# Tile 1's tokens and products behind two chunks of weights, the memory's loads on the weights' queue, products of ones between

## The chip, the cores and the metric

The kernel runs on one core of a Trainium2 chip. The metric is the device time of one execution in microseconds (us). The kernel before took a median of 922.51 us in three runs (921.90 to 922.72).

## The reference

The kernel computes two chained blocks of a transformer on 256 tokens of width 1024, in float32. The first block has two layers (a mixer of two kinds of attention, a SwiGLU with 2816 hidden columns, two layer norms in each). The second attends to its own tokens and to a memory of 256 rows. Only the first products and the memory's norm matter here:

```python
def _mixer_ab(h, w_in, q_norm, w_uq, kv_norm, w_ukv, sinks, w_out, cos, sin):
    B, S, _ = h.shape
    proj = jnp.einsum('bsd,df->bsf', h, w_in)
    c_q, c_kv, k_r, q_s, k_s, v_s = _split_cols(proj, AB_SPLITS)
    q = jnp.einsum('bsr,rf->bsf', _rms_norm(c_q, q_norm), w_uq).reshape(B, S, MLA_HEADS, MLA_NOPE + MLA_ROPE)
    ...

def first_block(x, ab_w_in, ...):
    for layer in range(DEPTH):
        ...
            mix = _mixer_ab(x, ab_w_in[i], ab_q_norm[i], ...)
        x = _layer_norm(DEEPNORM_ALPHA * x + mix, ln1_g[layer], ln1_b[layer])
        ffn = _swiglu(x, ffn_w_gate[layer], ffn_w_up[layer], ffn_w_down[layer])
        x = _layer_norm(DEEPNORM_ALPHA * x + ffn, ln2_g[layer], ln2_b[layer])
    return x

def second_block(x, mem, norm_g, mem_norm_g, ...):
        ...
        mem_n = rms_norm(mem, mem_norm_g[layer])
        out_c = memory_cross_attention(qc, mem_n, w_mem_kv[layer]) * jax.nn.silu(gc)
        ...
```

## The kernel before

SP's queue holds tile 0 of x, the identity, chunks 0 to 3, tile 1 of x (L515), then chunk 4 and the rest. GpSimd's queue holds what is needed later: behind chunk 3's high part the memory's gains (`mem_g`), the memory's rows (`mem`, 1024 KB), the low-rank gains (`gains`) and two head parameters; behind chunk 7's high part the table `swa` (1536 KB) and `rope`.

The memory's norm is made on ScalarE (L1403, L1404) and VectorE (L1845, L1846) while TensorE does the second step. On ScalarE it stands behind the high part of chunk 8. TensorE turns the normed memory's tile 0 behind chunk 7 and tile 1 behind chunk 8.

Of the kernel before, what the change touches and what calls it, by code (L numbers as in the profile page):

```python
# [28 lines left out]
P = 128  # L29
TT = 2  # L30
S = TT * P
D = 1024
# [232 lines left out]
def build_program(nc, d, out):  # L265
    with ExitStack() as ctx:
# [236 lines left out]
        def read(name, steps):  # L503

            u = PRODUCTS[name].u0 + steps - 1
            return acc_free[u % 2], TT * (u // 2 + 1)

        block = ctx.enter_context(nc.Block())

        @block.sync
        def _(sp):

            def load_x(t):
                sp.dma_start(x[:, t, :], d["x"][t * P:(t + 1) * P, :]).then_inc(loaded[f"x{t}"], 16)  # L515

            load_x(0)
# [19 lines left out]
            for g in PRODUCTS.values():  # L537
                if g.name[:2] == "up":
                    users = PRODUCTS["ukv" if g.name == "up0" else "down0"]
                    sp.wait_ge(chunk_used, users.c0 + users.steps * users.kc // users.kp)  # L540
                for n in range(g.steps * g.kc // g.kp):
                    if g.c0 + n:
                        load_chunk(g, n)
                    else:
                        for m, landed in enumerate((first_staged, staged[STAGE[0]])):
                            cut = slice(m * FIRST, (m + 1) * FIRST)
                            sp.dma_start(stage_of(0, WIDTH[0])[:, cut], d["w_ab_in"][0][:, cut]).then_inc(landed, 16)
                    if g.c0 + n == NS - 1:
                        load_x(1)
            for t in range(TT):  # L550
                for j in range(2):
# [9 lines left out]
        def _(pool):  # L561
            def load(name, dst, src):
                pool.dma_start(dst, src).then_inc(loaded[name], 16)

            def row(src, n):
                return bass.AP(tensor=src.tensor, offset=src.offset, ap=[[0, P], [1, n]])

            pool.memset(no_mask[:, :], 0.0).then_inc(constants_set, 1)
            pool.wait_ge(hi_done, NS)
            load("mem_g", row_g[:, :], row(d["mem_norm_g"], D))  # L570
            load("mem", mem_x, d["mem"].rearrange("(t p) n -> p t n", t=TT))
            load("gains", gains, row(d["gains"], Q_RANK + KV_RANK))
            load("heads", head_par[:, :, :].rearrange("p a h -> p (a h)"), row(d["head_par"], 16))
# [73 lines left out]
        def _(pe):  # L647
# [5 lines left out]
            def turn_part(part, name, src, ready):  # L653
# [7 lines left out]
                last.then_inc(turned, 1)  # L661

            def step(g, j, hi, lo, k0=0, turned_by=None, between=None, second=None):

                u, cps = g.u0 + j, g.kc // g.kp
                pair = u % 2
                passes = [(t,) for t in range(TT)] if second else [tuple(range(TT))]
                for tiles in passes:
                    if second:  # L670
                        second(tiles[0])
                    if u >= 2:

                        pe.wait_ge(acc_free[pair], 2 * (u // 2) - (tiles == (0,)))
                    for m in range(cps):
                        n = j * cps + m
# [554 lines left out]
        def _(act):  # L1231
# [224 lines left out]
            act.copy(w_hi(0, 0, FIRST), stage_of(0, FIRST)).then_inc(first_hi, 1)  # L1456
            turn_part(last, "x0")
            act.wait_ge(staged[STAGE[0]], 16)
            act.copy(w_hi(0, FIRST, FIRST), stage_of(0, WIDTH[0])[:, FIRST:]).then_inc(hi_done, 1)  # L1459
            done["chunks"] = 1  # L1460
            split_to(NS)
            turn("x0", xt_hi, 0, [1])

# [160 lines left out]
        def _(dve):  # L1624
# [348 lines left out]
            done["chunks"] = 1  # L1973
            turn_part(last, xt_hi, xt_lo, 0, "x0")
            split_to(NS)
            turn("x0", xt_hi, xt_lo, 0, [1])

# [340 lines left out]
```

## Time and profile before

| | |
|---|---|
| Median of 3 runs | 922.51 us (921.90 to 922.72) |
| The profiled execution | 924.75 us |
| Its span | 922.6 us |
| TensorE busy | 911.3 us, 99% of the span |
| VectorE busy | 608.7 us, 66% |
| ScalarE busy | 508.4 us, 55% |
| DMA, mean | 184 GB/s |

The rows of the trace are given in the section below. PE is TensorE, PEld its loading of stationary operands, DVE is VectorE, ACT ScalarE, POOL GpSimd and SP the engine that issues most transfers. A row of a timeline has the start and the duration in us, and a group "x8" covers eight records. For a product the duration runs to the modelled end of its pipeline, so in a dense stretch the distance from start to start is the one that counts. What stands in brackets is the idle time before it and what ended it. In a row of transfers the last number is the time from issue to landing in us.

### The profile page before, as it was taken

The numbers are of one execution on the slowest core, as the hardware profiler recorded it, in microseconds if no ns is written. First come the engines' busy times: TensorE is split into PE (matmuls) and PEld (weight loads), VectorE is DVE, ScalarE is ACT, GpSimd is POOL, SyncE is SP. The second block draws the span as 40 slices with busy tenths as digits, with TensorE's granted clock in tenths as the row PEclk, the third lists the DMA queues.
The fourth block names the chain that finished last, engine by engine and source line by source line (L and its number), as shares of the span: only waits on it lengthen the run. The fifth ranks groups of instructions, "written<-read, shape, count | busy, mean of one in ns | idle before, by whom it ended". The sixth has DMA issues, their size and how long they took to land.

```text
span 922.6 us, 12818 instructions
## 1 busy us (share of the span) xinstructions
PE 911.3 (99%) x4766; PEld 765.2 (83%) x4766; DVE 608.7 (66%) x1003; ACT 508.4 (55%) x819; POOL 36.4 (4%) x53
## 2 busy tenths in 40 slices
PE   8999999999999999999999999999999999999997
PEld 6888878888888898877888888887888888888876
DVE  3788687666662766778766666376656577574665
ACT  4876664555552456666455555355457574655444
POOL 1100024100000001000000000001000000000000
PEclk9999999999999999999999999999999999999999
DMA  8664466755574668444755557454564565545651
GB/s 293 238 220 121 122 226 194 262 183 185 192 246 131 146 172 256 137 155 166 256 176 187 195 189 245 125 198 142 185 204 137 160 195 167 163 152 189 197 174 64
DMA packets 72556, 169.39 MB, mean 184 GB/s; under 512 B 11304, under 2 KB 33216, under 8 KB 71856
## 3 DMA queue, kind: packets, MB, share of 16 engines
q1 hardware_dynamic: 69536, 155.83, 52.2%
q0 software_dynamic: 2816, 12.48, 4.1%
q8 instruction: 39, 0.64, 0.3%
q10 hardware_dynamic: 144, 0.26, 0.1%
q14 instruction: 21, 0.17, 0.1%
HBM read 167.49 MB, written 1.06 MB: 183 GB/s over the span
## 4 chain that ended last, share of the span: by engine, by line
PE 95%; DVE 2%; ACT 1%; DMA 1%; issue 0%; SPq 0%; ACTq 0%; DVEq 0%
PE psum L740 21%; PE psum L927 14%; PE psum L693 8%; PE psum L688 8%; PE psum L690 8%; PE psum L931 7%; PE psum L960 7%; PE psum L965 3%; PE psum L851 3%; PE psum L861 3%; PE psum L855 3%; PE psum L1062 2%; PE psum L1093 1%; PE psum L660 1%; PE psum L1076 1%; PE psum L1018 1%
## 5 line engine op out<-in xcount | busy, mean ns | idle before, releaser
L1636 DVE TENSOR_TENSOR base_lo<-stage,base_hi 128x1024 fp32r<-128x1024 f32 (+3 forms) x222 | 262.1, 1204 | 95.1 <-ACT base_hi L1245 94.2
L1245 ACT CAST base_hi<-stage 128x1024 fp32r<-128x1024 f32 (+3 forms) x222 | 223.8, 1035 | 52.4 <-PE psum L693 25.3
L1636 DVE TENSOR_TENSOR extra_lo<-stage,extra_hi 128x1024 fp32r<-128x1024 f32 (+1 forms) x68 | 80.0, 1202 | 47.5 <-ACT extra_hi L1245 47.4
L688 PE MATMUL psum<-base_hi,xt 128*128 128x512 f32 (+2 forms) x272 | 107.8, 396 | 1.6 <-ACT base_hi L1459 0.7
L690 PE MATMUL psum<-base_lo,xt 128*128 128x512 f32 (+2 forms) x272 | 105.2, 387 | 1.2 <-DVE base_lo L1636 0.7
L693 PE MATMUL psum<-base_hi,xt 128*128 128x512 f32 (+2 forms) x272 | 105.3, 387 | 0.0
L1245 ACT CAST extra_hi<-stage 128x1024 fp32r<-128x1024 f32 (+1 forms) x68 | 68.1, 1030 | 49.3 <-PE psum L740 33.5
L740 PE MATMUL psum<-base_hi,ht 128*128 128x512 f32 x288 | 87.3, 393 | 0.0
L927 PE MATMUL psum<-xt,extra_hi 128*128 128x512 f32 x320 | 87.3, 394 | 0.0
L960 PE MATMUL psum<-xt,base_hi 128*128 128x512 f32 x240 | 76.5, 403 | 0.0
L927 PE MATMUL psum<-xt,base_hi 128*128 128x512 f32 x256 | 69.7, 394 | 0.0
L740 PEld LDWEIGHTS psum<-base_hi,ht 128*128 128x128 f32 x288 | 53.7, 188 | 11.8 <-issue 0.5
L927 PEld LDWEIGHTS psum<-xt,extra_hi 128*128 128x128 f32 x320 | 55.4, 189 | 8.0
L688 PEld LDWEIGHTS psum<-base_hi,xt 128*128 128x128 f32 x272 | 51.5, 189 | 12.3 <-ACT base_hi L1459 1.1
L690 PEld LDWEIGHTS psum<-base_lo,xt 128*128 128x128 f32 x272 | 51.6, 190 | 11.7 <-DVE base_lo L1636 1.2
L693 PEld LDWEIGHTS psum<-base_hi,xt 128*128 128x128 f32 x272 | 51.4, 189 | 10.0 <-DVE xt L1677 0.4
L1436 ACT COPY qk_t<-psum 128x512 f32<-128x512 f32 x18 | 10.6, 587 | 84.4 <-PE psum L927 84.4
L1926 DVE TENSOR_TENSOR qk_t<-qk_t,psum 128x512 f32<-128x512 f32 x18 | 12.4, 687 | 62.9 <-ACT qk_t L1436 62.9
L931 PEld LDWEIGHTS psum<-xt,extra_lo 128*128 128x128 f32 x320 | 47.7, 189 | 5.9
L740 PE MATMUL psum<-base_lo,ht 128*128 128x512 f32 x144 | 50.8, 391 | 0.2 <-DVE base_lo L1636 0.2
L965 PEld LDWEIGHTS psum<-xt,base_lo 128*128 128x128 f32 x240 | 42.9, 188 | 9.2
L927 PEld LDWEIGHTS psum<-xt,base_hi 128*128 128x128 f32 x256 | 44.3, 189 | 6.5
(243 smaller groups left out, 1548.2 us busy)
## 6 DMA issues: line engine op xcount, KB each, us to landing
stage<-in_w_up SPq DMA_DIRECT2D x80, 512.0 KB, 4.5
stage<-in_w_down SPq DMA_DIRECT2D x44, 512.0 KB, 4.5
stage<-in_w_in_a SPq DMA_DIRECT2D x22, 512.0 KB, 4.9
stage<-in_w_cd_in SPq DMA_DIRECT2D x16, 512.0 KB, 4.7
stage<-in_w_in_b SPq DMA_DIRECT2D x12, 512.0 KB, 3.6
stage<-in_w_ab_in SPq DMA_DIRECT2D x11, 480.0 KB, 6.8
ln_par<-in_ln POOLq DMA_DIRECT2D x4, 1024.0 KB, 6.6
stage<-in_w_ab_out SPq DMA_DIRECT2D x8, 512.0 KB, 3.7
```

The lines of the kernel that those rows point to most:

```text
L688: pe.matmul(acc, ah, wh, start=(k == 0), stop=False)
L690: pe.matmul(acc, ah, wl, start=False, stop=False)
L693: last = pe.matmul(acc, al, wh, start=False, stop=(k == g.kc - 1))
L740: last = pe.matmul(psum[:, 2 * ((g.u0 + half) % 2) + t, :], a, w(c, half * 512, 512), start=(k == 0 and w is w_hi and a is ah), stop=summed)
L851: pe.matmul(acc, ah, w_hi(c, at, g.n), start=(k == 0), stop=False)
L855: pe.matmul(acc, al, w_hi(c, at, g.n), start=False, stop=False)
L927: last = pe.matmul(acc, w_hi(c, at, P), xt[:, k, :, :].rearrange("p a n -> p (a n)"), start=(k == 0), stop=(k == g.kc - 1))
L931: last = pe.matmul(acc[:, 0:S], w_lo(c, at, P), xt_hi[:, k, :], start=False, stop=False)
L960: last = pe.matmul(acc, w_hi(c, at, P), joint[:, k, :, :].rearrange("p a n -> p (a n)"), start=(k == 0), stop=(k == g.kc - 1))
L965: last = pe.matmul(acc[:, 0:S], w_lo(c, at, P), joint[:, k, 0, :], start=False, stop=False)
L1245: act.copy(w_hi(c, 0, w), stage_of(c, w)).then_inc(hi_done, 1)
L1636: dve.tensor_tensor(w_lo(c, 0, w), stage_of(c, w), w_hi(c, 0, w).bitcast(F32), ALU.subtract).then_inc(lo_done, 1)
```

## The change

Three parts, all within the first 30 us.

1. On SP's queue the load of tile 1 moves from behind chunk 3 to behind chunk 1. The three loads `mem_g`, `mem` and `gains` leave GpSimd's queue and stand on SP's behind chunk 7.
2. TensorE does chunks 0 and 1 for tile 0, turns tile 1, does chunks 0 and 1 for tile 1 (`early`), and then chunks 2 and 3 for both tiles together. Within `early` the products of the high weights (high and low tokens) stand ahead of those of the low weights, for each half of chunk 0 and for the whole of chunk 1. For tile 0 seven products of ones stand between: 0, 1 and 1 ahead of the low products of the three groups, 3, 2 and 0 behind them.
3. On ScalarE and VectorE the turn of tile 0's second half moves behind chunk 0 on ScalarE, and the two halves of tile 1's turn stand ahead of chunks 2 and 3 instead of behind chunk 3.

The whole diff:

```diff
--- before.py
+++ after.py
@@ -505,6 +505,9 @@
             u = PRODUCTS[name].u0 + steps - 1
             return acc_free[u % 2], TT * (u // 2 + 1)
 
+        def row(src, n):
+            return bass.AP(tensor=src.tensor, offset=src.offset, ap=[[0, P], [1, n]])
+
         block = ctx.enter_context(nc.Block())
 
 
@@ -513,6 +516,13 @@
 
             def load_x(t):
                 sp.dma_start(x[:, t, :], d["x"][t * P:(t + 1) * P, :]).then_inc(loaded[f"x{t}"], 16)
+
+            def load_memory():
+                for name, dst, src in (
+                        ("mem_g", row_g[:, :], row(d["mem_norm_g"], D)),
+                        ("mem", mem_x, d["mem"].rearrange("(t p) n -> p t n", t=TT)),
+                        ("gains", gains, row(d["gains"], Q_RANK + KV_RANK))):
+                    sp.dma_start(dst, src).then_inc(loaded[name], 16)
 
             load_x(0)
             sp.dma_start(ident[:, :], d["ident"]).then_inc(loaded["ident"], 16)
@@ -545,8 +555,10 @@
                         for m, landed in enumerate((first_staged, staged[STAGE[0]])):
                             cut = slice(m * FIRST, (m + 1) * FIRST)
                             sp.dma_start(stage_of(0, WIDTH[0])[:, cut], d["w_ab_in"][0][:, cut]).then_inc(landed, 16)
-                    if g.c0 + n == NS - 1:
+                    if g.c0 + n == 1:
                         load_x(1)
+                    if g.c0 + n == 2 * NS - 1:
+                        load_memory()
             for t in range(TT):
                 for j in range(2):
                     cut = slice(j * 512, (j + 1) * 512)
@@ -562,14 +574,8 @@
             def load(name, dst, src):
                 pool.dma_start(dst, src).then_inc(loaded[name], 16)
 
-            def row(src, n):
-                return bass.AP(tensor=src.tensor, offset=src.offset, ap=[[0, P], [1, n]])
-
             pool.memset(no_mask[:, :], 0.0).then_inc(constants_set, 1)
             pool.wait_ge(hi_done, NS)
-            load("mem_g", row_g[:, :], row(d["mem_norm_g"], D))
-            load("mem", mem_x, d["mem"].rearrange("(t p) n -> p t n", t=TT))
-            load("gains", gains, row(d["gains"], Q_RANK + KV_RANK))
             load("heads", head_par[:, :, :].rearrange("p a h -> p (a h)"), row(d["head_par"], 16))
             pool.wait_ge(hi_done, 2 * NS)
             load("swa", table, d["swa"])
@@ -660,19 +666,44 @@
                     last = pe.transpose(turn_bank(name, g)[:, k * P:(k + 1) * P], src(k0 + k, t), ident[:, :])
                 last.then_inc(turned, 1)
 
+            def early(g, pair, t, turned_by):
+
+                acc = psum[:, 2 * pair + t, 0:g.n]
+                for c, group, before_lows, behind in ((0, (0,), 0, 3), (0, (1,), 1, 2), (1, (0, 1), 1, 0)):
+                    ks = [(kk, c * g.kp + kk) for kk in group]
+                    at = lambda k: (slice(None), k, slice(t * P, (t + 1) * P))
+                    for kk, k in ks:
+                        pe.wait_ge(*((hi_done, c + 1) if k else (first_hi, 1)))
+                        pe.wait_ge(turn_hi, turned_at(turned_by, t, k))
+                        pe.matmul(acc, xt_hi[at(k)], w_hi(c, kk * g.n, g.n), start=(k == 0), stop=False)
+                    for kk, k in ks:
+                        pe.wait_ge(turn_lo, turned_at(turned_by, t, k))
+                        pe.matmul(acc, xt_lo[at(k)], w_hi(c, kk * g.n, g.n), start=False, stop=False)
+                    if t == 0:
+                        ones_by_ones(before_lows)
+                    for kk, k in ks:
+                        pe.wait_ge(*((lo_done, c + 1) if k else (first_lo, 1)))
+                        last = pe.matmul(acc, xt_hi[at(k)], w_lo(c, kk * g.n, g.n), start=False, stop=False)
+                    if t == 0:
+                        ones_by_ones(behind)
+                    elif ks[-1][0] == g.kp - 1:
+                        last.then_inc(chunk_used, 1)
+
             def step(g, j, hi, lo, k0=0, turned_by=None, between=None, second=None):
 
 
                 u, cps = g.u0 + j, g.kc // g.kp
                 pair = u % 2
-                passes = [(t,) for t in range(TT)] if second else [tuple(range(TT))]
-                for tiles in passes:
-                    if second:
-                        second(tiles[0])
+                passes = [(tuple(range(TT)), range(cps))]
+                if second:
+                    passes = [(tuple(range(TT)), range(2, cps))]
+                    for t in range(TT):
+                        second(t)
+                        early(g, pair, t, turned_by)
+                for tiles, chunks in passes:
                     if u >= 2:
-
-                        pe.wait_ge(acc_free[pair], 2 * (u // 2) - (tiles == (0,)))
-                    for m in range(cps):
+                        pe.wait_ge(acc_free[pair], 2 * (u // 2))
+                    for m in chunks:
                         n = j * cps + m
                         c = g.c0 + n
                         for kk in range(g.kp):
@@ -1454,12 +1485,16 @@
             turn_part(first, "x0")
             act.wait_ge(first_staged, 16)
             act.copy(w_hi(0, 0, FIRST), stage_of(0, FIRST)).then_inc(first_hi, 1)
-            turn_part(last, "x0")
             act.wait_ge(staged[STAGE[0]], 16)
             act.copy(w_hi(0, FIRST, FIRST), stage_of(0, WIDTH[0])[:, FIRST:]).then_inc(hi_done, 1)
             done["chunks"] = 1
+            turn_part(last, "x0")
+            split_to(2)
+            first, last = turn_parts("x0", [1])
+            turn_part(first, "x0")
+            split_to(3)
+            turn_part(last, "x0")
             split_to(NS)
-            turn("x0", xt_hi, 0, [1])
 
             def memory_norm():
                 act.wait_ge(constants_set, 3)
@@ -1972,8 +2007,12 @@
             split_first(1).then_inc(lo_done, 1)
             done["chunks"] = 1
             turn_part(last, xt_hi, xt_lo, 0, "x0")
+            split_to(2)
+            first, last = turn_parts("x0", [1])
+            turn_part(first, xt_hi, xt_lo, 0, "x0")
+            split_to(3)
+            turn_part(last, xt_hi, xt_lo, 0, "x0")
             split_to(NS)
-            turn("x0", xt_hi, xt_lo, 0, [1])
 
             def memory_norm():
                 dve.wait_ge(loaded["mem_g"], 16)
```

On TensorE before, the first step from its first product on; `base_hi` and `base_lo` are the weights' parts, `xt` the tokens, and the third row of each three takes the tokens' low part:

```order
L688 MATMUL psum<-base_hi,xt 128x480 [waits turn_hi,first_hi]
L690 MATMUL psum<-base_lo,xt 128x480 [waits first_lo]
L693 MATMUL psum<-base_hi,xt 128x480 [waits turn_lo]
L688 MATMUL psum<-base_hi,xt 128x480 [waits turn_hi,hi_done]
L690 MATMUL psum<-base_lo,xt 128x480 [waits lo_done]
L693 MATMUL psum<-base_hi,xt 128x480 [waits turn_lo]
...
L660 MATMUL psum<-ident,x 128x128 [waits turn_lo,loaded_x1]
L660 MATMUL psum<-ident,x 128x128 x3
```

On TensorE now, the same place; `qk_t` holds the ones:

```order
L678 MATMUL psum<-base_hi,xt 128x480 [waits turn_hi,first_hi]
L681 MATMUL psum<-base_hi,xt 128x480 [waits turn_lo]
L686 MATMUL psum<-base_lo,xt 128x480 [waits first_lo]
L1153 MATMUL psum<-qk_t 128x128 x3
...
L678 MATMUL psum<-base_hi,xt 128x480 [waits turn_hi,hi_done] x2
L681 MATMUL psum<-base_hi,xt 128x480 [waits turn_lo] x2
L1153 MATMUL psum<-qk_t 128x128
L686 MATMUL psum<-base_lo,xt 128x480 [waits lo_done] x2
L666 MATMUL psum<-ident,x 128x128 [waits turn_lo,loaded_x1]
L666 MATMUL psum<-ident,x 128x128 x3
```

The transposes of tile 1 stand behind 12 products instead of 24, and four products that need no low part of chunk 1 stand ahead of the wait for it.

On ScalarE before, from tile 0's first turn to the splitting of chunk 3:

```order
L1280 CAST xt<-psum 128x4x128 [waits turned]
L1456 CAST base_hi<-stage 128x480 [waits first_staged]
L1280 CAST xt<-psum 128x4x128 [waits turned]
L1459 CAST base_hi<-stage 128x480 [waits staged0]
L1245 CAST base_hi<-stage 128x960 [waits staged1]
L1245 CAST base_hi<-stage 128x960 [waits staged2]
L1245 CAST base_hi<-stage 128x960 [waits staged3]
L1280 CAST xt<-psum 128x4x128 [waits turned] x2
```

On ScalarE now:

```order
L1311 CAST xt<-psum 128x4x128 [waits turned]
L1487 CAST base_hi<-stage 128x480 [waits first_staged]
L1489 CAST base_hi<-stage 128x480 [waits staged0]
L1311 CAST xt<-psum 128x4x128 [waits turned]
L1276 CAST base_hi<-stage 128x960 [waits staged1]
L1311 CAST xt<-psum 128x4x128 [waits turned]
L1276 CAST base_hi<-stage 128x960 [waits staged2]
L1311 CAST xt<-psum 128x4x128 [waits turned]
L1276 CAST base_hi<-stage 128x960 [waits staged3]
```

Chunk 2 now stands behind the turn of tile 1's first half, and chunk 3 behind that of its second.

On SP now, the head of the queue (before, tile 1 stood behind the three chunks after chunk 0, and no row of the memory's was there):

```order
L557 DMA stage<-in_w_ab_in 128x480 x2
L545 DMA stage<-in_w_ab_in 128x960
L518 DMA x<-in_x 128x1024
L545 DMA stage<-in_w_ab_in 128x960 x2
L545 DMA stage<-in_w_ab_in 128x960 [waits lo_done] x4
L525 DMA row_g<-in_mem_norm_g 128x1024
L525 DMA arena<-in_mem 128x2x1024
L525 DMA arena<-in_gains 128x640
L545 DMA stage<-in_w_ab_in 128x960 [waits lo_done] x4
```

Chunk 8, the first of the last row, stands behind the memory's three loads.

## Rows read from the trace of the kernel before

**Rows 1.** The page, part 1 and the first line of part 4.

```profile
PE 911.3 (99%) x4766; PEld 765.2 (83%) x4766; DVE 608.7 (66%) x1003; ACT 508.4 (55%) x819; POOL 36.4 (4%) x53
...
PE 95%; DVE 2%; ACT 1%; DMA 1%; issue 0%; SPq 0%; ACTq 0%; DVEq 0%
```

**Rows 2.** TensorE's waits from 30 us on: total, times, longest, in us.

```profile
PE psum L1002 <- DVE pair_probs L1751: 0.6, 1, 0.6
PE psum L1043 <- DVE row_g L1986: 0.6, 1, 0.6
```

**Rows 3.** Windows: length, busy time of each engine, then PEclk, DMA share, GB/s.

```profile
4.70:7.00 2.30, 2.02 (x14) 1.68 (x13) 0.80 (x2) 1.42 (x3) 0.00 (x0) 1.00 0.98 310
7.00:12.00 5.00, 2.83 (x8) 1.22 (x8) 3.15 (x5) 2.85 (x5) 0.00 (x0) 0.99 0.99 365
12.00:15.40 3.40, 3.40 (x10) 2.83 (x10) 2.04 (x2) 0.86 (x1) 2.23 (x4) 0.51 0.79 261
...
12.00:18.00 6.00, 6.00 (x25) 5.04 (x24) 2.04 (x2) 1.13 (x2) 2.48 (x4) 0.72 0.73 254
```

**Rows 4.** Timeline of TensorE: start and duration in us, then idle before.

```profile
5.82 0.61 PE L1122 MATMUL psum<-qk_t 128*128 128x128 f32 x4
...
8.91 0.48 PE L688 MATMUL psum<-base_hi,xt 128*128 128x480 f32 x1 [0.69 <-ACT base_hi L1459]
9.60 0.48 PE L690 MATMUL psum<-base_lo,xt 128*128 128x480 f32 x1 [0.21 <-DVE base_lo L1965]
...
11.75 0.64 PE L690 MATMUL psum<-base_lo,xt 128*128 128x480 f32 x1 [0.71 <-DVE base_lo L1636]
...
17.10 1.04 PE L660 MATMUL psum<-ident,x 128*128 128x128 f32 x8
18.47 0.46 PE L688 MATMUL psum<-base_hi,xt 128*128 128x480 f32 x1 [0.33 <-ACT xt L1280]
...
19.10 0.49 PE L693 MATMUL psum<-base_hi,xt 128*128 128x480 f32 x1
19.43 0.38 PE L688 MATMUL psum<-base_hi,xt 128*128 128x480 f32 x1
...
24.01 0.37 PE L688 MATMUL psum<-base_hi,xt 128*128 128x480 f32 x1
...
34.39 1.04 PE L660 MATMUL psum<-ident,arena 128*128 128x128 f32 x8
```

**Rows 5.** Timeline of ScalarE: chunk 1, tile 1's turn, chunk 8.

```profile
9.51 0.99 ACT L1245 CAST base_hi<-stage 128x960 fp32r<-128x960 f32 x1 [0.65 <-DMA stage<-in_w_ab_in]
...
17.74 1.07 ACT L1280 CAST xt<-psum 128x512 fp32r<-128x512 f32 x2 [4.87 <-PE psum L660]
...
27.41 1.00 ACT L1245 CAST base_hi<-stage 128x960 fp32r<-128x960 f32 x1 [0.40 <-DMA stage<-in_w_ab_in]
```

**Rows 6.** Timeline of VectorE: chunks 1 to 3, tile 1's turn, the memory's first norm.

```profile
10.53 3.52 DVE L1636 TENSOR_TENSOR base_lo<-stage,base_hi 128x960 fp32r<-128x960 f32 x3 [0.39 <-ACT base_hi L1245]
18.35 1.29 DVE L1677 TENSOR_TENSOR xt<-psum,xt 128x512 fp32r<-128x512 f32 x2 [4.30 <-ACT xt L1280]
...
30.09 1.28 DVE L1846 SCALAR_TENSOR_TENSOR arena<-arena,rms_st,row_g 128x1024 f32<-128x1024 f32 x1
```

**Rows 7.** Issues on SP at 2.66, 4.08, 12.91, 27.34: KB, us to landing.

```profile
stage<-in_w_ab_in SPq DMA_DIRECT2D x1, 480.0 KB, 6.8
...
x<-in_x SPq DMA_DIRECT2D x1, 512.0 KB, 9.0
...
stage<-in_w_ab_in SPq DMA_DIRECT2D x1, 480.0 KB, 7.8
...
stage<-in_w_ab_in SPq DMA_DIRECT2D x1, 480.0 KB, 3.7
```

**Rows 8.** Timeline of GpSimd: issues of mem_norm_g and swa.

```profile
13.17 0.67 POOL L563 DMA_DIRECT2D row_g<-in_mem_norm_g  x1 [12.06 <-ACT base_hi L1245]
...
27.31 0.53 POOL L563 DMA_DIRECT2D arena<-in_swa  x1 [11.65 <-ACT base_hi L1245]
```

## Prediction

> **What bounds the kernel now.** I read part 1 of the page, then the chain that ended last, then the windows and timelines of the first 60 us, where every edit lies. TensorE is busy for 911.3 of 922.6 us and makes up 95% of the chain [rows 1]: a microsecond of its work brought forward shortens the run, if nothing behind it waits for something else. After 30 us its waits are 1.8 us in all, the longest 0.6 us each [rows 2] (three groups of 0.2 us each are not shown). So there is nothing to win there, and little that would swallow a gain. The first 24 us are different. TensorE records 2.83 busy us of 5.00 between 7 and 12 us. Then, from 12.0 to 15.4 us, it is busy throughout at a granted clock of 0.51, half speed, that is 1.2 instead of 2.4 GHz. Before 7 us it was busy 2.02 of 2.30 us at 1.00 [rows 3]. Up to 11.75 us the products wait for weights: 0.69, 0.21 and 0.71 us at 8.91, 9.60 and 11.75 us [rows 4]. The waits end when ScalarE has rounded a landed chunk and VectorE has made its rest.
>
> The measure is the start of the second step of ab_in, 24.01 us [rows 4]. A product at full speed takes (34.39 - 24.01)/48 = 0.216 us start to start [rows 4].
>
> **The first step in the old order.** At 11.75 us, when the low part of chunk 1 is there, 7 of the step's 48 products are done and 41 are left. The 17 of tile 0 take 17.10 - 11.75 = 5.35 us [rows 4]; at full speed they would take 17 x 0.216 = 3.68 us, and 0.11 us more since the first after a wait is followed at 0.33 and not 0.22 us (19.10 to 19.43) [rows 4]. So the half clock costs 5.35 - 3.79 = 1.56 us. Then eight transposes until tile 1's first product: 18.47 - 17.10 = 1.37 us. Its 24 products take 24.01 - 18.47 = 5.54 us, 0.35 us over 24 x 0.216 [rows 4].
>
> **The same step in the new order, part by part.**
> - High parts ahead of low, tile 0. In chunk 1 the two high products and the two of the tokens' rest need no low weights, so four and not one stand before the wait of 11.75 us. Nothing on VectorE moves ahead of that low part: it starts chunk 1 at 10.53 us as now [rows 6]. Ten products are done, 38 are left: 3 x 0.216 = 0.65 us saved.
> - Products of ones: seven, between the products, behind waits of tile 0. Two of them now are 4 records in 0.61 us [rows 4], so 0.3 us each at most. Three stand before 8.91, one before 9.60, two and one around chunk 1. The four early products of chunk 1 start from 10.55 to 11.2 us; the product of ones behind them is over by 11.75 us. I cost them at nothing; were each late by as much as its wait doesn't cover, the last alone would count, since each stage restarts from a weight: 0 to 0.3 us. What they may give is the clock. Busy time before the fall was 57% (2.83 of 5.00). With three more products and up to 7 x 0.3 = 2.1 us of ones it would be nearer the 88% of 4.7 to 7 us, which was followed by no fall [rows 3]. Bounds: 0 if the clock falls all the same, 1.56 if it does not fall. I take 1.56.
> - Tile 1's tokens behind chunk 1. The issue at 4.08 us landed 9.0 us later, at 13.1 us. Chunk 1 (2.66 + 6.8) landed at 9.46 us, so chunks 2, 3 and this tile came in 3.64 us, 1472 KB at 414 GB/s [rows 7]. Moved ahead of two of them the tile is there at about 10.8 us. Chunks 2 and 3 are 1.3 us later, 12.0 and 13.1. The transposes can start once the two low products of chunk 1 are out: 11.75 + 0.33 + 0.22 = 12.30 us; they don't wait for the load.
> - Tile 1's turn. By the distances of now (17.74, 18.47 and 19.10 against 17.10) [rows 4, 5] ScalarE copies the first half at 12.94, the first product starts at 13.67 and the one with the rest of the tokens at 14.30 us. Today a product with the low weights stands between these two; now the rest is needed second. It costs 14.30 - 13.67 - 0.216 = 0.41 and 0.11 behind it, 0.53 (unrounded) in place of 0.35: 0.18 us lost.
> - ScalarE and VectorE queues. ScalarE: tile 0's second half moves behind chunk 0 (a gap before the row of 9.51 us takes it [rows 5]), and chunk 2 stands behind the first turn: 13.5 to 14.4, turn to 14.9, chunk 3 to 15.9 us, against 12.86 us now. VectorE follows with 1.16 us a chunk (3.52 for three) and 0.65 a turn [rows 6]: chunk 2's rest at 15.65, turn 16.25, chunk 3's 17.35 us. TensorE reaches chunk 2 at 14.63 + 10 x 0.216 = 16.8 and chunk 3 at 19.4 us; both are covered, by 1.1 us or more.
>
> Sum: 11.75 + 38 x 0.216 + 0.11 + 1.37 + 0.53 = 21.98 us for the start of the second step; 24.01 - 21.98 = 2.03 = 0.65 + 1.56 - 0.18. The profiled execution took 924.75 us with a span of 922.6; the sum gives 920.6 for the span and 922.7 for that execution. It stood 2.2 us over the median of 922.51, and I take the difference off the median: **920.5 us**.
>
> On the clock there is a rule that speaks against carrying the 1.56 over. The Trainium skill, "TensorE: Matmul & The Clock Gate", Part 1, says that the gate runs free and isn't started by the kernel, so that the number of slow products differs from run to run. One trace can't show that; three times within 0.8 us don't contradict it. By the rule half of the fall, an estimate, might be what the median holds, and the sum would be 921.3.
>
> **The memory's three loads.** They leave GpSimd's queue (issued at 13.2 to 14.5 us) for the weights' queue, behind chunk 7 and ahead of chunk 8. Chunk 7's issue waits for VectorE's chunk 3, so 17.4 us, and its landing is 3.7 us later by the row of an issue into an idle queue [rows 7], 21.1 us. SP then issues mem_norm_g, mem, gains and chunk 8 without a wait that counts. Queued behind them are chunk 8 (480 KB) and all later weights. ScalarE must split chunk 8 before it squares mem: now chunk 8 lands at 27.41 and the first tile of mem is normed at 30.09 + 1.28 = 31.37 us, 3.96 us later [rows 5, 6]. TensorE takes it at 34.39 now [rows 4], 32.36 then. So chunk 8 may land as late as 28.4 us. What stands before its landing is 512 + 1024 + 320 + 480 = 2336 KB, 2.39 MB. At 414 GB/s it lands at 26.9 us; at 254 GB/s, the mean of 12 to 18 us [rows 3], at 30.5. How fast a row spread over 128 partitions goes on this queue no row shows. With the 1504 KB of mem and chunk 8 at 414 and the 832 KB of the two spread rows at 254 it is 28.2 us. I take 27.5, between the nearer two, as the weights' queue ran at 414 with several transfers waiting: in time by 0.9 us, cost 0. Bounds: 0 and 2.1 us.
>
> The Trainium skill, "DMA: Bandwidth & Descriptors", Specifications, puts a core's share of HBM at about 358 GB/s; the 414 GB/s above lies over it, and the measurement decides. By the page's figure chunk 8 would land at 27.8 us, an estimate, still in time.
>
> **The rivals.**
> - The clock falls all the same. For it: transposes and two waits at 12.3 to 14.3 us leave holes. Against: much more work before. Two low products, the transposes, and about five products would run at half speed, but the 0.6 us wait for the turn hides some: 0.3 us on the transposes and 0.4 to 0.7 on products. Less saved, 0.7 to 1.0: 921.2 to 921.5.
> - Chunk 8 is late. For it: one load issued at 12.91 us beside GpSimd's took 7.8 us [rows 7], and spread rows are untried here. It costs what it lands behind 28.4 us, and the transposes of mem after chunk 7 wait: with 28.7 to 30.5 us, 0.3 to 2.1 us, so 920.8 to 922.6.
> - Slower than before. The same place, with swa on top: chunk 7's split at 24.9 us (now 2.4 us later) lets GpSimd issue 1536 KB [rows 8], which then shares with chunk 8. At 254 GB/s the three loads end at 28.6 us and chunk 8 at half that rate 3.9 us later, 32.5: 4.1 us of stall, 924.6 us. It decides from a landing at 30.4 us on. Against it: 414 GB/s with a full queue.
> - The edit gives more: if the two waits around the turn shorten, or the fall costs more in other runs, 919.8.
>
> **How the numbers follow.** No change means within 0.2%, 1.85 us, so 920.66 to 924.36; it is about what a measurement here can tell. The forecast is near that edge.
> - Forecast, 920.5, own range 920.0 to 921.0: 0.48, of which 0.34 below the edge and 0.14 within.
> - Clock falls: 0.14, all within.
> - Chunk 8 late: 0.22, 0.02 below and 0.20 within.
> - Slower: 0.05. More gain: 0.07, below. The remaining 0.04, within: the gain is swallowed by later waits, up to the 1.8 us of [rows 2].
>
> Faster 0.43, same 0.52, slower 0.05. The range, 919.7 to 922.4, leaves out the slower rival and the ends of the others.
>
> **What would show it.** In the new profile: tile 1's eight transposes start near 12.3 us instead of 17.10; the granted clock stays 1.00 from 12 to 15.4 us and products follow at 0.22 us; tile 1's second product starts 0.6 us behind its first; the second step starts near 22.0 us. ScalarE's ninth chunk starts before 28.4 us, and the first transposes of mem stand right behind chunk 7's last product, near 32.4 us. A clock of 0.5 anywhere before 20 us speaks for the first rival; a gap before the transposes of mem for the second or third. The forecast is wrong if the second step starts later than 22.6 us, or if it starts near 22.0 and the span isn't shorter by about as much.

## The result, and the profile after

The changed kernel takes 925.24 us (median of 8 runs, 923.95 to 926.75) against 922.34 for the kernel before (8 runs, 921.73 to 922.98). The ratio is 1.0028, with a 95% interval of 1.0017 to 1.0038: slower, and outside the range of the prediction. The profiled execution took 924.95 us with a span of 923.0. One later execution of the kernel before took 1292 us at a granted clock of 0.655; no number below contains it.

The windows of the changed kernel: length, busy time of each engine, granted clock, DMA share, GB/s.

```profile
7.00:12.00 5.00, 5.00 (x33) 4.29 (x32) 2.74 (x4) 1.87 (x4) 0.00 (x0) 1.00 1.03 409
12.00:15.40 3.40, 2.89 (x14) 2.12 (x13) 2.68 (x4) 3.40 (x5) 0.34 (x1) 1.00 0.45 171
17.00:19.00 2.00, 2.00 (x10) 1.71 (x10) 1.37 (x2) 0.00 (x1) 0.00 (x0) 1.00 0.67 117
24.00:34.40 10.40, 8.90 (x45) 7.50 (x44) 5.29 (x7) 4.40 (x8) 1.07 (x2) 1.00 1.02 415
34.40:60.00 25.60, 23.95 (x155) 20.13 (x154) 22.01 (x60) 20.78 (x56) 3.51 (x6) 1.00 0.63 222
```

What TensorE does in the first 24 us is what was forecast. From 7 to 12 us it is busy for 5.00 of 5.00 us where it was busy for 2.83, and from 12 to 15.4 us the clock stays at 1.00 where it was at 0.51 [rows 3]. TensorE's timeline of the same trace (start, duration, form, idle before) stands against [rows 4]:

```profile
11.26 1.04 PE L666 MATMUL psum<-ident,x 128*128 128x128 f32 x8
12.63 0.46 PE L678 MATMUL psum<-base_hi,xt 128*128 128x480 f32 x1 [0.33 <-ACT xt L1311]
13.26 0.49 PE L681 MATMUL psum<-base_hi,xt 128*128 128x480 f32 x1 [0.18 <-DVE xt L1712]
...
20.96 0.38 PE L719 MATMUL psum<-base_hi,xt 128*128 128x480 f32 x1
...
33.04 1.09 PE L666 MATMUL psum<-ident,arena 128*128 128x128 f32 x8 [1.50 <-DVE arena L1881]
36.94 1.22 PE L666 MATMUL psum<-ident,arena 128*128 128x128 f32 x8 [0.19 <-DVE ht L1712]
40.63 0.82 PE L666 MATMUL psum<-ident,arena 128*128 128x128 f32 x6
41.82 0.49 PE L721 MATMUL psum<-base_lo,xt 128*128 128x480 f32 x1 [0.16 <-DVE base_lo L1671]
45.31 0.41 PE L1074 MATMUL psum<-ident,arena 128*128 128x128 f32 x2 [0.82 <-DVE row_g L2025]
```

The second step starts at 20.96 us, 3.05 us earlier than before. Of these, 1.03 us are no gain: chunk 1 happened to be rounded at 8.48 us in this execution, at 9.51 in the old one. Counted from there it is 12.48 us, by the forecast 21.98 - 9.51 = 12.47. But from 24 us on TensorE is busy for 1.5 us less of 10.4, and the memory's transposes, which had no wait, wait for 1.50 us. What holds them stands on ScalarE. Its timeline, start and duration:

```profile
21.16 1.02 ACT L1453 COPY arena<-psum 128x480 f32<-128x480 f32 x2 [4.15 <-PE psum L724]
22.06 1.90 ACT L1276 CAST base_hi<-stage 128x960 fp32r<-128x960 f32 x2
29.02 1.00 ACT L1276 CAST base_hi<-stage 128x960 fp32r<-128x960 f32 x1 [5.06 <-DMA stage<-in_w_ab_in]
29.92 1.06 ACT L1434 ACTIVATE arena<-arena 128x1024 f32<-128x1024 f32 x1
...
33.67 1.00 ACT L1276 CAST base_hi<-stage 128x960 fp32r<-128x960 f32 x1 [0.91 <-DMA stage<-in_w_ab_in]
34.57 1.01 ACT L1453 COPY arena<-psum 128x480 f32<-128x480 f32 x2
```

ScalarE sits idle for 5.06 us until chunk 8 lands at 29.0 us, where the squares of mem are queued behind it. Then it waits again, 0.91 us for chunk 9, with the copy of the second step's result and the turn of mem queued behind that. In the chain that ended last DMA's share rose from 1 to 4% [rows 1]:

```profile
PE 90%; DMA 4%; DVE 3%; ACT 2%; issue 1%; SPq 0%; ACTq 0%; DVEq 0%
```

The issues on SP, with KB and us to landing, are chunk 6 (14.59 us), chunk 7 (16.26), mem_norm_g, mem, gains and chunk 8 (18.2):

```profile
stage<-in_w_ab_in SPq DMA_DIRECT2D x1, 480.0 KB, 3.4
...
stage<-in_w_ab_in SPq DMA_DIRECT2D x1, 480.0 KB, 5.7
...
row_g<-in_mem_norm_g SPq DMA_DIRECT2D x1, 512.0 KB, 7.3
...
arena<-in_mem SPq DMA_DIRECT2D x1, 1024.0 KB, 9.4
...
arena<-in_gains SPq DMA_DIRECT2D x1, 320.0 KB, 9.8
...
stage<-in_w_ab_in SPq DMA_DIRECT2D x1, 480.0 KB, 10.8
```

Chunk 7 needs 5.7 us where 3.7 was assumed [rows 7]: it is down at 22.0 us and not at 20.0. In two microseconds of this time the transfers ran at 117 GB/s (window 17 to 19). The four behind it need 7.0 us for 2.39 MB, 340 GB/s.

### The profile page after: what moved, and what is told of

Its sections match the earlier page's. It is cut to its first block, busy times and chain, and to the rows that moved or that the text cites. A ratio compares the mean times of both kernels' runs of the same rounds, so it can differ in the third digit from the quotient of the medians.

```text
span 923.0 us, 12846 instructions
## 1 busy us (share of the span) xinstructions
PE 911.1 (99%) x4780; PEld 765.5 (83%) x4780; DVE 608.8 (66%) x1003; ACT 508.1 (55%) x819; POOL 34.1 (4%) x50
## 4 chain that ended last, share of the span: by engine, by line
PE 90%; DMA 4%; DVE 3%; ACT 2%; issue 1%; SPq 0%; ACTq 0%; DVEq 0%
PE psum L771 21%; PE psum L958 14%; PE psum L962 7%; PE psum L719 7%; PE psum L724 7%; PE psum L721 7%; PE psum L991 6%; PE psum L996 3%; PE psum L882 3%; PE psum L886 3%; PE psum L892 3%; DMA stage<-in_w_cd_in 2%; DVE base_lo L1671 2%; PE psum L1093 2%; DMA stage<-in_w_ab_in 2%; PE psum L1124 1%
## 5 line engine op out<-in xcount | busy, mean ns | idle before, releaser
L719 PE MATMUL psum<-base_hi,xt 128*128 128x512 f32 (+2 forms) x264 | 103.8, 393 | 0.0
L721 PE MATMUL psum<-base_lo,xt 128*128 128x512 f32 (+2 forms) x264 | 101.4, 384 | 0.2 <-DVE base_lo L1671 0.2
L724 PE MATMUL psum<-base_hi,xt 128*128 128x512 f32 (+2 forms) x264 | 101.5, 384 | 0.0
L721 PEld LDWEIGHTS psum<-base_lo,xt 128*128 128x128 f32 x264 | 49.6, 188 | 9.7 <-DVE base_lo L1671 0.6
L719 PEld LDWEIGHTS psum<-base_hi,xt 128*128 128x128 f32 x264 | 49.6, 188 | 9.4 <-issue 0.4
L724 PEld LDWEIGHTS psum<-base_hi,xt 128*128 128x128 f32 x264 | 49.6, 188 | 9.4
```

Source lines behind the costliest of these rows:

```text
L719: pe.matmul(acc, ah, wh, start=(k == 0), stop=False)
L721: pe.matmul(acc, ah, wl, start=False, stop=False)
L724: last = pe.matmul(acc, al, wh, start=False, stop=(k == g.kc - 1))
```

## The experiments

To compare executions I count from the start of chunk 1's rounding on ScalarE. In the profiles it lies between 7.97 and 9.51 us, and in the two of the unchanged kernel at 9.51 and 8.56, so most of this comes from nothing in the code. **D1** runs to the copy of the first step's result (ScalarE), **D2** to the memory's first transposes, **D3** to the transposes at L1074 of the changed kernel (45.31 us above). "Wait" is TensorE's before D2. The last column is the median less that of the kernel before in the same batch. `head_par` is the 8 KB load of the head parameters on GpSimd's queue, issued behind chunk 3's high part.

| kernel | D1 | D2 | wait | D3 | median | difference |
|---|---|---|---|---|---|---|
| before, again | 14.71 | 24.89 | 0 | 35.82 | 922.48 | -0.20 |
| e2 old order, memory behind chunk 7 | 13.16 | 23.33 | 0 | 34.28 | 922.76 | +0.08 |
| e8 old order, memory behind chunk 3 | 14.70 | 24.88 | 0 | 35.83 | 922.85 | +0.28 |
| the change | 12.68 | 24.56 | 1.50 | 36.83 | 925.24 | +2.90 |
| e3 no ones | 12.64 | 24.64 | 1.66 | 36.94 | 925.25 | +2.57 |
| e5 swa later | 13.07 | 24.45 | 0.99 | 35.69 | 924.00 | +1.42 |
| e11 head_par later | 13.14 | 23.90 | 0.41 | 35.14 | 924.06 | +1.73 |
| e1 memory on GpSimd | 12.98 | 23.20 | 0 | 34.14 | 923.02 | +0.34 |
| e7 memory behind chunk 8 | 13.01 | 23.24 | 0 | 35.17 | 922.66 | +0.08 |
| e4 memory behind chunk 3 | 12.72 | 22.90 | 0 | 33.85 | 922.54 | -0.04 |
| e6 the same, no ones | 12.67 | 22.90 | 0 | 33.85 | 922.11 | -0.47 |
| e10 e6 once more | 12.68 | 22.90 | 0 | 33.85 | 922.20 | -0.37 |
| e9 e6, swa later | 12.66 | 22.84 | 0 | 33.78 | 922.21 | -0.36 |
| e12 e9, head_par later | 12.68 | 22.85 | 0 | 33.80 | 921.72 | -0.61 |

**The kernel before, unchanged.** 

> The kernel before, unchanged, to see its spans and clocks over several executions. Theory A (the profiled execution of before was a slow one: its span of 922.6 us holds a clock fall of 1.56 us that most executions have less of): most spans are 920 to 921 us and the granted clock of several is above 0.997. Theory B (all executions have the fall): the clocks are alike at 0.997 and the spans 920 us differ from 922.6 for another reason. Both expect a ratio of 1.000.

Measured 922.48 us (ratio 0.9996, 0.9987 to 1.0005). Theory A holds: ten of the twelve spans are 920.0 to 920.7 us, with mean clocks of 0.998 to 1.000; the other two are 922.0 and 923.0 us, with 0.997. The profiled execution is one of these two and had the fall, the stretch at about half clock, again:

```profile
12.00:15.40 3.40, 3.40 (x11) 2.86 (x10) 1.14 (x1) 0.00 (x0) 2.49 (x4) 0.58 0.83 280
```

**The three loads back on GpSimd.** `load_memory()` leaves SP; the three `load(...)` lines return ahead of `load("heads", ...)`.

> The changed kernel with the memory's three loads back on GpSimd's queue behind chunk 3's high part. Late-memory theory (chunk 8 landed at 29.0 us behind the three loads, the memory's norm came 1.5 us late for TensorE and all of the first step's 3 us were gone by 34 us): chunk 8 lands before 25 us, no wait before the transposes of the memory, and the time is 920 to 922.5 us. Rival (what is lost lies after 34 us, in the chains of the first heads, or in how the products are ordered): within 0.5 us of the changed kernel, 925 us.

Measured 923.02 us (1.0003, 0.9994 to 1.0011). The wait of 1.50 us is gone, and with it 2.6 of the 2.9 us of difference: the place of the loads made most of the loss. It isn't faster than before, though.

**Only the three loads moved, old order.**

```diff
 (kernel before)
+                    if g.c0 + n == 2 * NS - 1:
+                        load_memory()
```

> The kernel before with only the three loads moved to the weights' queue behind chunk 7, whose issue is at 14.1 us there. Late-memory theory in its narrow form (the loads hurt because chunk 7's issue is late and the first step ends early): no harm here, 922.3 us within 0.7, since chunk 8 is issued at 22.6 us anyway. Rival (the spread rows are slow on this queue and hold the weights up): chunk 8 lands at 28 us or later and the time is 923.5 to 925.

Measured 922.76 us (1.0003, 0.9991 to 1.0014): in the old order the same place costs nothing that shows. There chunk 7 is issued 4.6 us after chunk 1's rounding starts (13.19 less 8.63) and in the change 7.8 us after it (16.26 less 8.48), since there chunks 2 and 3 are split behind the turn of tile 1 and chunk 7's issue waits for chunk 3's low part. So the loads behind chunk 7 have 3.2 us less in the change. Chunk 8 is rounded at 27.36 us. And this execution of the old order, with no products of ones, had no fall:

```profile
12.00:15.40 3.40, 3.40 (x20) 2.96 (x20) 1.16 (x1) 0.09 (x1) 0.68 (x1) 1.00 0.81 260
...
17.00:19.00 2.00, 2.00 (x11) 1.72 (x10) 0.27 (x2) 1.00 (x1) 0.00 (x0) 1.00 0.92 354
```

Against the kernel before again D2 is 24.89 - 23.33 = 1.56 us shorter, the price forecast for the fall. (It is the only profile of the old order without a fall.) But the medians don't differ.

**The change without its seven products of ones.** Both calls of `ones_by_ones` in `early` leave.

> The changed kernel without the seven products of ones. Late-memory theory: TensorE loses up to 1.6 us in the first step if the clock falls, but the wait for the memory swallows it: within 0.5 us of the changed kernel's 925.2. Rival (the ones cost: they stand ahead of products): 922 to 924.

Measured 925.25 us (1.0023, 1.0012 to 1.0035), clock 1.00 throughout, 1.66 us of wait. So the clock stays up without the ones. What they cost can't be seen in these two kernels, since the wait for the memory swallows it.

**The loads right behind chunk 3.** `2 * NS - 1` becomes `NS - 1` in the condition of `load_memory()`.

> The changed kernel with the memory's three loads on the weights' queue right behind chunk 3 (issued before 6 us, without a wait), so that they take the 12 to 15 us in which the transfers stood idle. Late-memory theory: mem is there before 19 us, chunk 4 lands near 18 us (TensorE needs it at 21), chunk 8 before 25 us; nothing waits for the memory and the time is 2.8 us under the changed kernel, 922.4, or up to 0.5 less, as the first step in the new order is worth 0.2 to 0.5 us over the old one without a clock fall. Rival (the spread rows on this queue hold the weights up wherever they stand): chunk 4 lands after 21 us, TensorE waits, 923.5 or more.

Measured 922.54 us (0.9994, 0.9984 to 1.0005): the 2.9 us of difference are gone. ScalarE goes from chunk 6 to 8 without a wait, and the idle stretch of the change is filled:

```profile
12.00:15.40 3.40, 2.89 (x14) 2.11 (x13) 2.70 (x4) 2.74 (x4) 0.35 (x1) 1.00 1.03 411
17.00:19.00 2.00, 2.00 (x11) 1.72 (x11) 0.00 (x0) 1.00 (x1) 0.00 (x0) 1.00 1.01 400
```

**swa and rope two chunks later.** `pool.wait_ge(hi_done, 2 * NS)` becomes `2 * NS + 2`.

> The changed kernel with GpSimd's loads of swa and rope behind chunk 9's high part instead of chunk 7's. Two-part theory: 1.1 us of the 2.8 are the wait for the memory's norm, the other 1.4 us come from chunk 9, which landed at 33.6 us because swa (1536 KB) took three quarters of the transfers from 28 to 32 us, and which stands ahead of step 2's evacuation on ScalarE. So the second part goes: chunk 9 lands before 31 us and the time is 923.6 to 924.2. Rival (chunk 9 is late only because it stands behind the memory's loads and chunk 8): chunk 9 still after 32.5 us, within 0.4 of the changed kernel's 925.2.

Measured 924.00 us (1.0012, 1.0001 to 1.0024): the difference is 1.5 us less. Chunk 8 is as late as before (28.97), but chunk 9, which landed near 30.4 us (forecast: before 31), is not waited for:

```profile
28.97 1.00 ACT L1276 CAST base_hi<-stage 128x960 fp32r<-128x960 f32 x1 [4.55 <-DMA stage<-in_w_ab_in]
...
32.61 0.98 ACT L1276 CAST base_hi<-stage 128x960 fp32r<-128x960 f32 x1
```

What swa did there stands in the change's DMA queues from 28 to 29 us (q0 carries swa, q1 the weights; packets, MB, share of the 16 engines):

```profile
q0 software_dynamic: 30, 0.37, 86.7%
q1 hardware_dynamic: 34, 0.12, 28.2%
```

Both moved about as many packets, but one of swa had 12 KB, one of the weights 3.5. The Trainium skill, "DMA: Bandwidth & Descriptors", Queues, rings and completion order, says that an engine goes round its queues packet by packet; the trace agrees, 30 packets beside 34.

**Early loads and no ones.** e4 and e3 together.

> As e4_memory_early, without the seven products of ones, so that the wait for the memory hides nothing. Theory that the ones matter only in executions in which the clock falls: the median within 0.4 us of e4_memory_early, and among its executions one or two of twelve about 2 us over the others, as the kernel before has them. Rival (they keep the clock up in all): 1.5 us slower than e4_memory_early.

Measured 922.11 us (0.9987, 0.9976 to 0.9999), 0.43 us under e4, at the edge of the 0.4 that the theory allowed. One of the twelve executions (924.20 us, mean clock 0.996) stands 2 us over the rest. So the rival falls; that the ones matter in executions with a fall is not shown by this either.

**The loads behind chunk 8.** `2 * NS - 1` becomes `2 * NS`.

> The changed kernel with the memory's three loads behind chunk 8 instead of ahead of it. If it is chunk 8's split that holds the memory's norm up: chunk 8 lands before 25 us and the norm waits only for mem, so the wait before the transposes of the memory is under 0.5 us (1.5 in the changed kernel), and the time is 924.0 to 924.7, as chunk 9 stays late. If it is the bytes of mem themselves: mem lands at 28 us or later, the wait stays over 1 us and the time is 925.2.

Measured 922.66 us (0.9999, 0.9985 to 1.0012). Neither theory's time came out: both said 924.0 us or more. Chunk 8 is in time and mem, landing at 27.8 us, just so, with no wait before its transposes. Chunk 9 is late by 1.42 us in the profiled execution, which costs at 43.68 us. That execution (924.04) was 1.4 us over the median; whether the others have a late chunk 9 is not shown, so D3 may overstate this kernel.

**The old order with early loads.** As e2, with `NS - 1`.

> The kernel before with one thing changed: the memory's three loads on the weights' queue, behind tile 1's tokens (so behind chunk 3), and no new order of the first products. Theory A (the 0.1 to 0.4 us between the old and the new order, read from the split of chunk 1 to the first transposes of mem, are real and are all that the new order gives): those transposes 23.3 us behind the split of chunk 1, and a median 0.1 to 0.4 us over that of the new order with early loads, 922.3 to 922.9. Theory B (the 0.3 to 0.5 us by which early loads stood under before come from the loads, which then wait for nothing, and the order gives nothing): a median of 922.1 to 922.4, equal to the new order's. Rival C: chunks 4 and 5, behind 1.9 MB of other loads, now stall the old order, which takes chunk 2 earlier: over 923.

Measured 922.85 us (1.0005, 0.9996 to 1.0013), 0.65 to 0.74 over the same loads in the new order (e6, e10). Four of its twelve executions have a mean clock of 0.997 or less; the median of the other eight is 922.74, still 0.54 to 0.64 over those of e6 and e10 taken the same way. So the new order gives something of its own, and theory B falls. D1 without a fall says 13.16 - 12.67 = 0.49 us.

**Early loads, no ones, swa later; and e6 once more.**

> The changed kernel without its seven products of ones, with the memory's loads behind chunk 3 and the load of swa and rope two chunks later. Theory A (swa costs only where chunk 8 or 9 is late; with early loads neither is): the same as without the later table, within 0.3 us, 922.0 to 922.5. Rival B (swa slows the chunks of the second step even with early loads): chunk 9's rounding on ScalarE earlier, waits at 42, 44 and 55 us gone, 0.5 to 1 us less, 921.3 to 921.8. Rival C (swa comes late for its own use): over 923, with a wait for table.

> The same kernel as e6_early_no_ones once more: the changed kernel without its seven products of ones and with the memory's loads behind chunk 3. If its 0.13% under before is real, the median is again 0.2 to 0.7 us under that of before and the interval of the ratio lies under 1; if it was chance, the interval takes in 1.

Measured 922.21 (0.9996, 0.9987 to 1.0005) and 922.20 us (0.9991, 0.9983 to 1.0000). So swa is harmless here once no chunk is late, as theory A has it. The repeated e6 lies where its expectation put it, but its interval ends at 1.0000: a gain of 0.1% is likely, not certain.

**head_par later.** `load("heads", ...)` goes behind `load("rope", ...)`, once in the change and once in e9.

> The changed kernel with the 8 KB load of head_par not at chunk 4's time but behind swa and rope, at about 25 us (it is first used at 50 us). In the profile of the change the transfers fell to 122 and 112 GB/s at 17 to 19 us, just while GpSimd's queue moved head_par's small packets; chunk 7 then landed 5.7 us behind its issue. Theory A (head_par's packets, spread over 128 partitions, made that slump): 250 GB/s or more at 17 to 19 us, chunk 7 down about 1.3 us earlier (near 20.7 us), chunk 8's rounding at 27.7 us and not 29.0, no wait before the first transposes of mem, and a median 1 to 1.8 us less, 923.4 to 924.2. Rival B (the slump is of the weights' queue itself, as it starts the two spread rows behind a queue that had run empty): the slump stays, chunk 8 at 28.8 to 29.2 us, a median of 924.9 to 925.5. Rival C: head_par's packets make the same slump at their new time, 27 to 29 us, where chunks 8 and 9 land: 925.5 to 927.

> The kernel of e9_early_table_later (memory's loads behind chunk 3, swa and rope two chunks later, no products of ones) with head_par behind rope too. In its chain nothing waited for a load after 22 us, so theory A (no landing is on the path): the same, 921.9 to 922.5. Rival B (chunks 6 and 7, which ScalarE waited for by 0.2 to 0.3 us, hold the second step): 0.2 to 0.5 less, 921.6 to 922.0.

Measured 924.06 (1.0022, 1.0013 to 1.0032) and 921.72 us (0.9992, 0.9983 to 1.0001). Chunk 7 is issued 0.3 us later in e11 (16.56 for 16.26 us), so windows have to be counted from its issue. The second microsecond behind it, and the first five, without head_par's packets (e11), with chunk 7's landing:

```profile
17.56:18.56 1.00, 1.00 (x6) 0.88 (x5) 1.00 (x2) 0.00 (x0) 0.00 (x0) 1.00 0.68 124
16.56:21.56 5.00, 5.00 (x25) 4.37 (x24) 2.11 (x2) 0.88 (x2) 0.00 (x0) 1.00 0.85 273
...
stage<-in_w_ab_in SPq DMA_DIRECT2D x1, 480.0 KB, 4.6
```

and the same windows of the change, where the landing took 5.7 us:

```profile
17.26:18.26 1.00, 1.00 (x6) 0.88 (x5) 1.00 (x2) 0.00 (x0) 0.00 (x0) 1.00 0.51 68
16.26:21.26 5.00, 5.00 (x25) 4.32 (x24) 2.11 (x2) 0.85 (x2) 0.00 (x0) 1.00 0.76 215
```

Neither theory alone: by the one profile without it here, this 8 KB load made 1.1 us of chunk 7's delay (e3, e5 and e7, which have it too, took 5.8, 5.6 and 6.0 us), but a lull to 124 GB/s is there without it. Nor do the spread rows of rival B make it. In e7 they are issued only at 18.07 us, behind chunk 8, and the second microsecond behind chunk 7's issue (17.63 to 18.63) is at 95 GB/s all the same. Chunk 8 is rounded 0.66 us sooner after chunk 1 (19.88 for 20.54 us), a wait of 0.41 us is left before the memory's transposes, and the median is 1.2 us lower. e12's time is the one that its rival B named, but D2 and D3 are those of e9 (22.85 and 33.80 for 22.84 and 33.78 us), so no shorter path shows.

**How often the clock falls.** The profiles with the fall had a mean granted clock of 0.997, those without 0.998 to 1.00. By this mark, which doesn't say where in an execution the clock fell, 22 of 150 executions in the old order (before, e0, e2, e8) had a fall and 4 of 117 in the new. Within the new order it is 2 of 65 with ones and 2 of 52 without. So the new order itself makes the fall rarer, and the ones show no part in it.

## Why the prediction was wrong

**The clock: the step "I take the difference off the median" failed.** The fall was read rightly and its price too: 1.56 us forecast, 1.56 measured (D2 of before again and of e2). But by the mean clock only one in eight executions of before has a fall (16 of 126), and the profiled one was among them. That and its late chunk 1 are why it stood 2.2 us over the median: e0's profiled execution, with the same fall, took 924.13 us, and less 1.56 us that is its median (922.48) within 0.1 us; in before's, chunk 1 came 0.95 us later still. The median holds no fall, so there was nothing to take off. The profile's excess was set down as a mere offset and then the fall subtracted on top, which counts it twice. The prediction cited a rule against exactly this step. The Trainium skill, "TensorE: Matmul & The Clock Gate", Part 1, says that the gate runs free, so that the number of slow products differs from run to run. The runs agree (16 of 126), and by them it should have had the whole term and not half: 922.51 - 0.47 = 922.0, were all else right.

**The order of the first products: right.** +0.65 for three products and -0.18 for the waits made 0.47 us; D1 gives 0.49 us in the five profiles without ones (12.64 to 12.68 against 13.16). The medians agree with the size: the four kernels without ones and without a late load stand at -0.36 to -0.61, though only e6's interval lies under 1 and e10's ends at 1.0000.

**The products of ones: taken at 0, bound 0.3 us, measured up to 0.46.** In four of six profiles with ones (e1, e5, e7, e11) D1 is 12.98 to 13.14, in the other two 12.68 and 12.72. TensorE's timeline of e11 shows ones between products that wait for nothing:

```profile
8.93 0.38 PE L680 MATMUL psum<-base_hi,xt 128*128 128x480 f32 x1
9.14 0.38 PE L1152 MATMUL psum<-qk_t 128*128 128x128 f32 x2
9.28 0.47 PE L685 MATMUL psum<-base_lo,xt 128*128 128x480 f32 x1
9.59 0.61 PE L1152 MATMUL psum<-qk_t 128*128 128x128 f32 x4
9.95 0.68 PE L677 MATMUL psum<-base_hi,xt 128*128 128x480 f32 x2
```

Chunk 1's high weights were rounded at 9.28 us and its products began at 9.95; without ones they begin at about 1.05 us after the start of the rounding (e6: 9.47 for 8.43), here 1.66. That takes most of the 0.49 us back, and is a likely part of why e1 and e4 are not clearly below before. The medians of e4 and e6 differ by 0.4 us, but their D1 by 0.05 only, so the size in the median stays open.

**Chunk 8: the step "I take 27.5" failed.** It landed at 29.0 us, and with chunk 1 rounded 1.03 us sooner than in the trace of before the limit was about 27.5, not 28.4. So the stall was 1.50 us, inside the bound of 2.1 that belonged to the rival "chunk 8 is late". Counted from the issue in this trace the forecast was 16.26 + 3.7 + 6.4 = 26.4 us, 2.6 us too early. Of these, 0.6 are the four loads behind chunk 7, 7.0 us instead of 6.4: the price of 414 GB/s was right only from 23 us on (415 in the window from 24 us). The other 2.0 us came before, in the term "3.7 us later by the row of an issue into an idle queue": chunk 7 took 5.7 us. head_par's 8 KB make 1.1 of them (e11: 4.6 us). The other 0.9 stay open; they lie in the lull to 124 GB/s that e11 keeps, some 3 us behind the issue of chunk 6, before which the queue had been empty.

**Chunk 9: not in the sum at all.** The rival "slower" had swa sharing with chunk 8; it hit chunk 9 above all, and chunk 8 by some 0.4 us (10.8 us from issue to landing, 10.4 in e5). Counted from chunk 1, the change is behind e6 by 1.66 us at D2 (1.50 of it the wait) and by 2.98 at D3; by the last column it is 3.4. The last 1.3 us come behind chunk 9: its landing holds ScalarE's copy, the turn of mem and the low-rank norms, and so the waits at 36.94, 41.82 and 45.31 us. Taking swa out (e5) shortens D3 by 1.1 us and D2 by 0.1. Read against the rows: from one chunk being late I priced one wait and forgot that the next chunk's landing is queued on the same engine ahead of three more hand-overs.

**The balance.** Order +0.5 us gained, fall 0 in the median, late chunks 3.0 us lost (D3 of the change less e6): 2.5 us slower by this, 2.9 measured. Between the forecast of 2.0 us less and the 2.9 more lie 4.9 us: 1.56 are the fall, 2.98 the late chunks, and some 0.4 are not accounted for. Of the forecast's two tests for being wrong it was "starts near 22.0 and the span isn't shorter by about as much" that came out.

## What to carry to other kernels

Before a stall of the profiled execution is taken off a median, ask what the profiled execution stands above it: if the excess is as large as the stall, the median may not hold it. A load that moves into a weights' queue can make more than the next chunk late, each with its own engine and hand-overs: here chunks 8 and 9. And what it costs depends on when the queue reaches it: in the old order, 3.2 us earlier, the same place cost nothing that shows (e2). Put such loads where the queue runs empty: the same three loads cost 2.9 us more behind chunk 7 than behind chunk 3 (the change and e4). The best version here (e12: early loads, no ones, swa and head_par later) is at 921.72 us, ratio 0.9992 with an interval up to 1.0001. Only e6's interval, up to 0.9999, lies under 1. So the best that is left of the change is a gain of about 0.1%, likely but hardly shown.

## What the hardware showed unexpectedly

An 8 KB load spread over 128 partitions held up a 480 KB load on another queue by 1.1 us: with it all transfers ran at 215 GB/s over the five microseconds behind the issue of chunk 7, without it at 273 (change and e11). Beside a full queue in e6 it did no such thing (400 and 392 GB/s while its packets went, 18 to 20 us). A queue whose packets are 12 KB took three quarters of the engines' time from one with 3.5 KB packets (86.7% beside 28.2% from 28 to 29 us). And the same program has its clock fall in some executions and not in others. In the three profiles with the fall (before, e0, e8) it costs 1.54 to 1.56 us against e2; the 22 executions of the old order with a low mean clock stand 2.1 us over the others in the median, so the price need not be the same in all.
